# Six different starting addresses for the slots of two weight rings in a two-block forward pass

## The chip, the cores and the metric

The kernel runs on one core of one Trainium2 chip. The metric is device time of one launch in microseconds. One profiled execution is read beside it.

## The reference

Two transformer-like blocks are applied to 256 tokens of width 1024, all in float32. Cut to what matters:

```python
# first block
h = rmsnorm(x, pre_mix_norm);  proj = h @ w_in                 # 1024 x 9792
y_ssd  = ssd_branch(z, xbc, dt, ...) @ w_ssd_out               # conv, two-direction scan, gated norm
y_attn = window_attention(q, k, v, ...) @ w_attn_out
x = x + rmsnorm((g_ssd * y_ssd + g_attn * y_attn) @ w_o)
f = square(relu(rmsnorm(x) @ w_mlp_in)) @ w_mlp_out            # 1024 x 4096, 4096 x 1024
x = x + rmsnorm(f)
# second block
proj = rms_norm(x) @ w_in_2                                    # 1024 x 5120
y_a = neighbourhood_attention(q, k, v) @ w_attn_branch;  y_b = short_gated_conv(cb, cc, ch) @ w_conv_branch
x = x + (sigmoid(ga) * y_a + sigmoid(gb) * y_b) @ w_o
x = x + square(relu(rms_norm(x) @ w_mlp_in)) @ w_mlp_out
```

## The kernel before

All weights come from HBM as 147 pieces (slots 0 to 146 of one list), each 128 partitions by 2048 float32 values, so 8192 bytes in a partition. SyncE fetches them in order into a ring of three tiles `raw`. For each piece ScalarE writes the rounded part `w_hi` (an ACTIVATE with Copy into the type fp32r, line 752), and VectorE writes the rest `w_lo = raw - w_hi` (line 1087). Both parts have a ring of three slots, and piece s uses slot s % 3 of each. ScalarE may write slot s % 3 when TensorE is done with piece s - 3; VectorE and ScalarE are two pieces ahead of TensorE (`AHEAD`).

TensorE takes the pieces in order (`stream`, line 346 in `three`). Each product of full precision is three matmuls in fp32r that add up in PSUM: hi by hi, hi by lo, lo by hi. There are two roles:

- "feat" pieces (q, xbc, mi, cb2, cc2, ch2, mi2 and half of kv): the weights are the stationary operand, 128 by 128, and the activations `ht_hi`/`ht_lo` move, 256 columns. 48 matmuls a piece.
- "tok" and "acc" pieces (z, gate, q2, k2, v2, g2, and ao, so, wo, mo, ab2, cv2, wo2, mo2): the activations are stationary, 128 by 128, and the weights move, 512 columns. 24 matmuls a piece.

The one piece "dt" has stationary weights of 64 columns, eight blocks of 256 bytes one behind the other.

In the profile a matmul is named by its moving operand first: `ps<-ht_hi,w_hi` moves ht_hi over stationary w_hi, and `ps<-w_hi,ff_hi` moves w_hi over stationary ff_hi.

The order of all work is written out by hand in one program per engine, and semaphores are waited for at constants. Every tile in SBUF has an address that is written out too: `at(name, shape, offset)` puts it at that many bytes of a partition beyond a common base, which is 16512 (128 modulo 512). In what follows the residue of a tile is its offset modulo 512; the common base adds the same 128 to all. `raw`, `w_hi`, `w_lo`, `ht_hi`, `ht_lo`, `ot_*`, `yt_*`, `ff_*` and `o2_*` have residue 0, and every block of 128 columns that TensorE takes from them starts at residue 0 again (in "dt" alternately at 0 and 256). `co_hi` and `co_lo`, the gated convolution that is the stationary operand of the two pieces cv2 (slots 109 and 110 of the list), have residue 64: their offsets are 153664 and 157760. These two are the only operands of line 346 that aren't at residue 0.

Of the kernel before, what the change touches and what calls it, by code (L numbers as in the profile page):

```python
# [26 lines left out]
F32R = mybir.dt.float32r  # L27
# [4 lines left out]
P = 128  # L32
TOK = 256
RT = TOK // P
D = 1024
# [6 lines left out]
PER_GROUP = HEADS // GROUPS  # L42
GW = D_INNER // GROUPS
# [4 lines left out]
XROW = TOK + 2 * PAD  # L48
Q_HEADS = 16
# [3 lines left out]
REL_W = 512  # L53
LOG1P_TERMS = 8

HEADS2 = 8
# [3 lines left out]
XROW2 = TOK + 2  # L60

RAW_RING = 3
SPLIT_RING = 3
AHEAD = 2
PIECE = 2048
# [37 lines left out]
PARAM_COLS = sum(w for _, w in PARAMS)  # L103
# [31 lines left out]
def build(nc, w_stream, w_dt, x_in, params_in, table_in, onehot_in, gate_bias_in, post_in, rpb_in,  # L135
# [3 lines left out]
    with ctx:  # L139
# [3 lines left out]
        def at(name, shape, offset, dt=F32):  # L143
            return nc.alloc_sbuf_tensor_at(name, shape, dt, offset=base + offset)

        raw = [at(f"raw{i}", [P, PIECE], 8192 * i) for i in range(RAW_RING)]
        w_hi = [at(f"w_hi{i}", [P, PIECE], 24576 + 8192 * i, F32R) for i in range(SPLIT_RING)]
        w_lo = [at(f"w_lo{i}", [P, PIECE], 49152 + 8192 * i, F32R) for i in range(SPLIT_RING)]

        params = at("params", [P, PARAM_COLS], 73728)  # L150

        def param(name):
            first, width = PARAM_AT[name]
# [12 lines left out]

        quad = param("quad")

        top = [73728 + 4 * PARAM_COLS]

        def scratch(name, shape):
            n = 1
            for s in shape[1:]:
                n *= s
            start = (top[0] + 31) // 32 * 32
            top[0] = start + 4 * n
            return at(name, shape, start)
# [11 lines left out]
        gstat = scratch("gstat", [P, 3, RT * GROUPS])  # L189
        hstat = scratch("hstat", [P, 3, 2 * RT * HEADS2])  # L190
        y_off = scratch("y_off", [P, RT, GW])
        junk = at("junk", [P, GW], 157760)
        assert top[0] <= 83968, top[0]

        ht_hi = at("ht_hi", [P, 8, TOK], 83968, F32R)
        ht_lo = at("ht_lo", [P, 8, TOK], 92160, F32R)
        ot_hi = at("ot_hi", [P, 8, TOK], 100352, F32R)
        ot_lo = at("ot_lo", [P, 8, TOK], 108544, F32R)
        x = at("x", [P, RT, D], 100352)
        g_post = at("g_post", [P, 2, D], 108544)  # L200
        bc = at("bc", [P, 16, TOK], 116736)
        btok = at("btok", [P, RT, 1024], 133120)
        conv_in = [at(f"conv_in{i}", [P, 4, XROW], 141376 + 8256 * i) for i in range(2)]
        conv_acc = [at(f"conv_acc{i}", [P, 4, TOK], 141376 + 8256 * i + 4160) for i in range(2)]
        xtok = at("xtok", [P, RT, D_INNER], 159584)
        dtw = at("dtw", [P, 6, RT, 2 * HEADS], 159584)
        dt_feat = at("dt_feat", [P, TOK], 162656)
        x_first = at("x_first", [P, RT, D], 116736)

        bias1 = at("bias1", [P, Q_HEADS, BIAS_W], 175968)  # L210
        q_t = at("q_t", [P, 8, TOK], 200544)
        k_t = at("k_t", [P, 2, TOK], 208736)
        v_tok = at("v_tok", [P, RT, 256], 210784)
        logit1 = [at(f"logit1_{i}", [P, 4, TOK], 116736 + 4096 * i) for i in range(2)]
        prob_t1 = [at(f"prob_t1_{i}", [P, RT, 4, P], 124928 + 4096 * i) for i in range(2)]
        onehot = at("onehot", [33, REL_W], 133120)
        table = at("table", [33, Q_HEADS], 135168)
        rel_row = at("rel_row", [Q_HEADS, REL_W], 137216)

        zg = at("zg", [P, RT, D_INNER], 175968)  # L220
        gates = at("gates", [P, RT, 2 * D], 192352)
        decay = [at(f"decay{i}", [P, PER_GROUP, P], 141376 + 2048 * i) for i in range(2)]
        step_w = [at(f"step_w{i}", [P, PER_GROUP, P], 145472 + 2048 * i) for i in range(3)]
        step_tmp = at("step_tmp", [P, PER_GROUP, P], 151616)
        cb = at("cb", [P, RT, P], 153664)

        adt_wide = at("adt_wide", [P, 4, 4, HEADS], 175968)
        cum_hi = at("cum_hi", [P, 4, P], 178016, F32R)
# [1 line left out]
        cum_sign = at("cum_sign", [P, 4, P], 182112)  # L230
        cum = at("cum", [P, 4, P], 198496)
        cum_l = [at("cum_l0", [P, 2, PER_GROUP, P], 194400, F32R), at("cum_l1", [P, 2, PER_GROUP, P], 202592, F32R)]
        cum_s = [at("cum_s0", [P, 4, P], 206688, F32R), at("cum_s1", [P, 4, P], 155712, F32R)]
        state = at("state", [P, 2, GW], 208736)
        x_state = at("x_state", [P, 2, GW], 210784)
        yt_hi = at("yt_hi", [P, 16, TOK], 116736, F32R)
        yt_lo = at("yt_lo", [P, 16, TOK], 133120, F32R)

        ff_hi = at("ff_hi", [P, 32, TOK], 116736, F32R)
        ff_lo = at("ff_lo", [P, 32, TOK], 149504, F32R)  # L240
        hn = at("hn", [P, RT, D], 198656)
        ff_tmp = [at(f"ff_tmp{i}", [P, 512], 206848 + 2048 * i) for i in range(2)]

        qk2 = at("qk2", [P, RT, 1024], 116736)
        v2 = at("v2", [P, RT, 512], 124928)
        qk2_t = at("qk2_t", [P, 8, TOK], 129024)
        cb2 = at("cb2", [P, 4, TOK], 137216)
        cc2 = at("cc2", [P, 4, TOK], 141312)
        acc2 = at("acc2", [P, 4, TOK], 145408)
        z2 = at("z2", [P, 4, XROW2], 149504)  # L250
        co_hi = at("co_hi", [P, 4, TOK], 153664, F32R)
        co_lo = at("co_lo", [P, 4, TOK], 157760, F32R)
        logit2 = [at(f"logit2_{i}", [P, 4, TOK], 161856 + 4096 * i) for i in range(2)]
        prob_t2 = [at(f"prob_t2_{i}", [P, RT, 4, P], 170048 + 4096 * i) for i in range(2)]
        bias2 = at("bias2", [P, RT, HEADS2, TOK], 178240)
        gates2 = at("gates2", [P, RT, 2 * D], 194624)
        o2_hi = at("o2_hi", [P, 4, TOK], 108544, F32R)
        o2_lo = at("o2_lo", [P, 4, TOK], 112640, F32R)
        scale_wide = at("scale_wide", [P, RT, P], 198656)
        scale_row = at("scale_row", [P, 2, TOK], 199680)  # L260

        ps = ctx.enter_context(nc.psum_tensor("ps", [P, 8, 512], F32))

# [1571 lines left out]
```

How the kernel before makes its waits and increments, by code:

```python
        def ready(eng, key):  # L307
            eng.wait_ge(*where[key][2])
# [1 line left out]
        def emptied(eng, key):  # L311
            eng.wait_ge(drained[where[key][0]], where[key][1] + 1)
# [13 lines left out]
            def claim(key, b):  # L327
                if uses[b]:
                    pe.wait_ge(drained[b], uses[b])
                where[key] = [b, uses[b], None]
                uses[b] += 1
# [22 lines left out]
            def stream(s):  # L355
                name, form, chunk, part, opens, closes = slots[s]
                hi, lo = w_hi[s % SPLIT_RING], w_lo[s % SPLIT_RING]
                pe.wait_ge(lo_ready, s + 1)
                if form == "acc":
                    a_hi, a_lo = gathered[name]
                    for n in range(2):
# [70 lines left out]
            def norm_turn(j):  # L432
                if j == 0:
                    pe.wait_ge(hn_ready, 2)
                for n in range(2):
                    if j in (1, 2):
                        pe.wait_ge(x_ready, 4 * j - 2 + 2 * n)
                    if j == 3:
                        emptied(pe, ("wo2", n, 0)), emptied(pe, ("wo2", n, 1))
                    turn_pairs(f"norm{j}", x_first if j == 0 else x, 2, 2 * n)
# [1 line left out]
            def mix_turn(j):  # L443
                src = gates if j == 0 else gates2
                for q in range(4):
                    if q % 2 == 0:
                        pe.wait_ge(mixed_ready, 4 * j + 2 * (q // 2 + 1))
                    turn_pairs(f"mix{j}", src, 1, q)
# [49 lines left out]
            def conv_turn(c):  # L499
                pe.wait_ge(conv_silu, c + 1)
                for r in range(RT):
```

## Time and profile before

| | |
|---|---|
| median of 3 runs | 1021.15 us (1018.06 to 1024.70) |
| span of the profiled execution | 1021.7 us |
| TensorE busy | 969.4 us, 95% |
| VectorE, ScalarE, GpSimd busy | 666.1, 524.4, 208.7 us |
| mean granted TensorE clock | 0.975 |
| bytes moved | 166.54 MB, mean 163 GB/s |

The span reaches from the first to the last instruction of the program in the one execution that was profiled; it is 0.6 us above the median of the runs. Matmuls overlap in the pipeline, so the busy time of one (284 or 390 ns) is longer than the distance from its start to the next one's, and only that distance says how fast TensorE works.

### The profile page before, as it was taken

How to read it: one execution, taken by the hardware profiler on the slowest of the kernel's cores; microseconds unless marked ns; L12 is line 12 of the kernel's file. 1: busy time of each engine (PE TensorE's matmuls, PEld its weight loads, DVE VectorE, ACT ScalarE, POOL GpSimd, SP SyncE). 2: the span in 40 equal slices, each digit the busy share in tenths (PEclk: the TensorE clock that was granted, in tenths of full speed). 3: DMA queues.
4: the chain of work that ended last, by engine and by line, in shares of the span. 5: the costliest groups of instructions: out<-in, count | busy, mean ns of one | idle time of the engine just before them, and what ended most of it. 6: DMA issues, size and time to landing. Idle time of an engine off the chain costs nothing.

```text
span 1021.7 us, 13780 instructions
## 1 busy us (share of the span) xinstructions
PE 969.4 (95%) x5726; PEld 849.9 (83%) x5726; DVE 666.1 (65%) x746; ACT 524.4 (51%) x660; POOL 208.7 (20%) x184
## 2 busy tenths in 40 slices
PE   5999998897988999998999999899999999999998
PEld 5997887876766788888999888789988889999887
DVE  4378876978898966467666444686764766565442
ACT  6457885564653564346555433555564345545331
POOL 0005566858887000000000000430000000000000
PEclk9999998998898999998999999899999999999999
DMA  8743223342221538543545555655336345555551
GB/s 314 261 166 120 87 84 124 124 165 62 83 82 52 216 124 302 198 173 140 178 165 192 199 188 205 160 210 181 122 115 233 134 165 206 180 195 200 177 197 41
DMA packets 24974, 166.54 MB, mean 163 GB/s; under 512 B 2938, under 2 KB 3066, under 8 KB 6224
## 3 DMA queue, kind: packets, MB, share of 16 engines
q1 hardware_dynamic: 22320, 156.12, 42.9%
q0 software_dynamic: 2592, 9.54, 3.3%
q8 instruction: 45, 0.74, 0.3%
q14 instruction: 17, 0.14, 0.0%
HBM read 164.57 MB, written 1.08 MB: 162 GB/s over the span
## 4 chain that ended last, share of the span: by engine, by line
PE 72%; DVE 13%; POOL 6%; issue 6%; ACT 3%; DMA 0%; SPq 0%; DVEq 0%; ACTq 0%; POOLq 0%
PE ps L346 65%; DVE w_lo L1087 2%; PE ps L528 2%; POOL conv_acc L1679 2%; POOL y_off L1677 2%; DVE step_w L1303 2%; PE ps L428 2%; DVE conv_acc L1263 2%; POOL logit L1666 1%; DVE decay L1308 1%; DVE xtok L1284 1%; DVE xtok L1340 1%; PE ps L459 1%; PE ps L494 1%; ACT w_hi L752 1%
## 5 line engine op out<-in xcount | busy, mean ns | idle before, releaser
L1087 DVE TENSOR_TENSOR w_lo<-raw,w_hi 128x2048 fp32r<-128x2048 f32 (+1 forms) x147 | 343.5, 2342 | 222.8 <-ACT w_hi L752 222.8
L752 ACT ACTIVATE w_hi<-raw 128x2048 fp32r<-128x2048 f32 (+1 forms) x147 | 279.5, 1904 | 212.9 <-PE ps L346 212.4
L346 PE MATMUL ps<-ht_hi,w_hi 128*128 128x256 f32 x952 | 274.4, 288 | 2.4 <-DVE ht_lo L1125 2.2
L346 PE MATMUL ps<-ht_lo,w_hi 128*128 128x256 f32 x952 | 272.1, 286 | 0.0
L346 PE MATMUL ps<-ht_hi,w_lo 128*128 128x256 f32 x952 | 271.9, 286 | 0.0
L346 PEld LDWEIGHTS ps<-ht_hi,w_hi 128*128 128x128 f32 x952 | 185.0, 194 | 5.5 <-DVE ht_lo L1125 2.8
L346 PEld LDWEIGHTS ps<-ht_lo,w_hi 128*128 128x128 f32 x952 | 185.0, 194 | 0.0
L346 PEld LDWEIGHTS ps<-ht_hi,w_lo 128*128 128x128 f32 x952 | 184.8, 194 | 0.0
L346 PE MATMUL ps<-w_hi,ht_hi 128*128 128x512 f32 (+1 forms) x320 | 126.6, 396 | 0.4 <-DVE w_lo L1087 0.2
L346 PE MATMUL ps<-w_hi,ht_lo 128*128 128x512 f32 (+1 forms) x320 | 123.9, 387 | 0.0
L346 PE MATMUL ps<-w_lo,ht_hi 128*128 128x512 f32 (+1 forms) x320 | 123.9, 387 | 0.0
L346 PE MATMUL ps<-w_hi,ff_hi 128*128 128x512 f32 x256 | 99.8, 390 | 0.0
L346 PE MATMUL ps<-w_lo,ff_hi 128*128 128x512 f32 x256 | 99.7, 390 | 0.0
L346 PE MATMUL ps<-w_hi,ff_lo 128*128 128x512 f32 x256 | 99.7, 390 | 0.0
L346 PEld LDWEIGHTS ps<-w_hi,ht_hi 128*128 128x128 f32 x320 | 60.9, 190 | 12.9 <-issue 0.7
L346 PEld LDWEIGHTS ps<-w_hi,ht_lo 128*128 128x128 f32 x320 | 60.6, 189 | 12.3
L346 PEld LDWEIGHTS ps<-w_lo,ht_hi 128*128 128x128 f32 x320 | 60.9, 190 | 11.8
L346 PEld LDWEIGHTS ps<-w_hi,ff_lo 128*128 128x128 f32 x256 | 48.1, 188 | 10.0
L346 PEld LDWEIGHTS ps<-w_hi,ff_hi 128*128 128x128 f32 x256 | 48.1, 188 | 9.9
L346 PEld LDWEIGHTS ps<-w_lo,ff_hi 128*128 128x128 f32 x256 | 48.1, 188 | 9.8
L1721 POOL MEMSET z<- 128x4 f32 x2 | 0.1, 104 | 253.3 <-PE ps L346 253.3
L1263 DVE SCALAR_TENSOR_TENSOR conv_acc<-conv_in,params,conv_acc 128x256 f32<-128x256 f32 x96 | 48.2, 548 | 1.0
(231 smaller groups left out, 1257.1 us busy)
## 6 DMA issues: line engine op xcount, KB each, us to landing
raw<-in_w_stream SPq DMA_DIRECT2D x146, 1024.0 KB, 4.8
bias<-rel_scratch POOLq DMA_DIRECT2D x1, 3072.0 KB, 16.0
bias<-in_rpb POOLq DMA_DIRECT2D x16, 128.0 KB, 4.2
gates<-in_gate_bias POOLq DMA_DIRECT2D x2, 768.0 KB, 5.0
x_first<-in_x_in SPq DMA_DIRECT2D x2, 512.0 KB, 4.0
x<-in_x_in POOLq DMA_DIRECT2D x1, 1024.0 KB, 7.3
g_post<-in_post POOLq DMA_DIRECT2D x2, 512.0 KB, 10.1
out_y<-x SPq DMA_DIRECT2D x4, 256.0 KB, 2.0
```

The lines of the kernel that those rows point to most:

```text
L346: ins = pe.matmul(o, still, moving, start=first and n == 0, stop=last and n == 2, skip_group_check=True)
L428: ins = pe.transpose(ps[:, b, i * TOK + r * P:i * TOK + r * P + P], source[:, r, f:f + P], ident)
L459: ins = pe.matmul(ps[:, 4 + h // 2, (h % 2) * TOK:(h % 2) * TOK + TOK], qa[rs, (1 - r) * P:(1 - r) * P + P], ka[rs, :], start=True, stop=True)
L494: ins = pe.matmul(ps[e * HD:e * HD + HD, 7, (h // 2) * P:(h // 2) * P + P], v2[:, jt, head * HD:head * HD + HD], prob_t2[a % 2][:, jt, pla ...
L528: ins = pe.matmul(ps[:, 4, o:o + HD], decay[c][:, h, :], xtok[:, c, f:f + HD], start=True, stop=True)
L752: act.activation(w_hi[s % SPLIT_RING][:, 0:width(s)], raw[s % RAW_RING][:, 0:width(s)], ACT.Copy).then_inc(hi_ready, 1)
L1087: dve.tensor_tensor(w_lo[s % SPLIT_RING][:, 0:width(s)], raw[s % RAW_RING][:, 0:width(s)], w_hi[s % SPLIT_RING][:, 0:width(s)].bitcast(F32 ...
L1263: ins = dve.scalar_tensor_tensor(conv_acc[k][:, i, :], conv_in[k][:, i, tap:tap + TOK], conv_w[:, tap, f:f + 1], conv_acc[k][:, i, :], ALU ...
L1284: link(dve.tensor_tensor(v, v, per_head(param("d_skip")[:, 4 * g:4 * g + 4], 4), ALU.mult))
L1303: ins = dve.tensor_tensor(w[:, :, :], w[:, :, :], cb[:, c, :].unsqueeze(1).to_broadcast([P, PER_GROUP, P]), ALU.mult)
L1677: link(pool.tensor_scalar(part, conv_in[k][:, 3, tap:tap + TOK], conv_w[:, tap, f:f + 1], None, ALU.mult))
L1679: ins = pool.tensor_tensor(conv_acc[k][:, 3, :], conv_acc[k][:, 3, :], part, ALU.add)
```

## The change

Only addresses are changed. The instructions of every engine, their order and their waits are the same as before. The slots of `w_hi` start 8256 bytes apart in place of 8192, those of `w_lo` 8288, and `w_lo` begins 192 bytes later. All tiles behind them up to offset 159584 and many beyond it move up by 512 bytes, so their residue stays. In the ring of `raw` nothing changes.

| slot | w_hi before | w_hi now | w_lo before | w_lo now |
|---|---|---|---|---|
| 0 | 0 | 0 | 0 | 192 |
| 1 | 0 | 64 | 0 | 288 |
| 2 | 0 | 128 | 0 | 384 |

The table gives the residues modulo 512. The activations of line 346 stay at 0, and `co_hi`, `co_lo` at 64.

```diff
         raw = [at(f"raw{i}", [P, PIECE], 8192 * i) for i in range(RAW_RING)]
-        w_hi = [at(f"w_hi{i}", [P, PIECE], 24576 + 8192 * i, F32R) for i in range(SPLIT_RING)]
-        w_lo = [at(f"w_lo{i}", [P, PIECE], 49152 + 8192 * i, F32R) for i in range(SPLIT_RING)]
-
-        params = at("params", [P, PARAM_COLS], 73728)
+        w_hi = [at(f"w_hi{i}", [P, PIECE], 24576 + (8192 + 64) * i, F32R) for i in range(SPLIT_RING)]
+        w_lo = [at(f"w_lo{i}", [P, PIECE], 49152 + 192 + (8192 + 96) * i, F32R) for i in range(SPLIT_RING)]
+
+        params = at("params", [P, PARAM_COLS], 74240)
...
-        ht_hi = at("ht_hi", [P, 8, TOK], 83968, F32R)
-        ht_lo = at("ht_lo", [P, 8, TOK], 92160, F32R)
+        ht_hi = at("ht_hi", [P, 8, TOK], 84480, F32R)
+        ht_lo = at("ht_lo", [P, 8, TOK], 92672, F32R)
...
-        ff_hi = at("ff_hi", [P, 32, TOK], 116736, F32R)
-        ff_lo = at("ff_lo", [P, 32, TOK], 149504, F32R)
+        ff_hi = at("ff_hi", [P, 32, TOK], 117248, F32R)
+        ff_lo = at("ff_lo", [P, 32, TOK], 150016, F32R)
...
-        co_hi = at("co_hi", [P, 4, TOK], 153664, F32R)
-        co_lo = at("co_lo", [P, 4, TOK], 157760, F32R)
+        co_hi = at("co_hi", [P, 4, TOK], 154176, F32R)
+        co_lo = at("co_lo", [P, 4, TOK], 158272, F32R)
```

## Rows read from the trace of the kernel before

**Rows 1.** The page, parts 1 and 4: busy time, and the chain by engine

```profile
PE 969.4 (95%) x5726; PEld 849.9 (83%) x5726; DVE 666.1 (65%) x746; ACT 524.4 (51%) x660; POOL 208.7 (20%) x184
...
PE 72%; DVE 13%; POOL 6%; issue 6%; ACT 3%; DMA 0%; SPq 0%; DVEq 0%; ACTq 0%; POOLq 0%
```

**Rows 2.** The chain in order of time: start us, us, what

```profile
23.40 37.47 PE ps L346 x312
...
82.12 1.89 POOL logit L1666
85.01 2.74 POOL conv_acc L1679
...
379.52 55.80 PE ps L346 x246
...
470.93 180.25 PE ps L346 x1152
```

**Rows 3.** Line 346 alone in three stretches: us, PE busy (matmuls), PEld busy, clock, DMA

```profile
0.00:61.00 61.00, 45.30 (x360) 44.92 (x360) 1.00 0.74 274
61.00:343.00 282.00, 156.15 (x985) 140.39 (x985) 0.93 0.30 105
343.00:1021.70 678.70, 634.26 (x3624) 557.50 (x3624) 0.99 0.51 177
```

**Rows 4.** Timeline, TensorE, a "feat" piece of mi: start us, us

```profile
499.86 0.28 PE L346 MATMUL ps<-ht_hi,w_hi 128*128 128x256 f32 x1
...
500.94 0.28 PE L346 MATMUL ps<-ht_hi,w_hi 128*128 128x256 f32 x1
```

**Rows 5.** Timeline, TensorE, pieces ab2: first and last of 48 matmuls

```profile
789.28 0.39 PE L346 MATMUL ps<-w_hi,o_hi 128*128 128x512 f32 x1
...
799.94 0.39 PE L346 MATMUL ps<-w_hi,o_lo 128*128 128x512 f32 x1
```

**Rows 6.** Timeline, TensorE, pieces cv2: the first four and the last of 48

```profile
800.16 0.40 PE L346 MATMUL ps<-w_hi,co_hi 128*128 128x512 f32 x1
800.40 0.39 PE L346 MATMUL ps<-w_lo,co_hi 128*128 128x512 f32 x1
800.63 0.40 PE L346 MATMUL ps<-w_hi,co_lo 128*128 128x512 f32 x1
800.86 0.39 PE L346 MATMUL ps<-w_hi,co_hi 128*128 128x512 f32 x1
...
811.13 0.39 PE L346 MATMUL ps<-w_hi,co_lo 128*128 128x512 f32 x1
```

**Rows 7.** Timeline, TensorE, the piece dt (stationary weights of 64 columns)

```profile
52.57 0.28 PE L346 MATMUL ps<-ht_hi,w_hi 128*64 128x256 f32 x1
...
52.91 0.28 PE L346 MATMUL ps<-ht_hi,w_hi 128*64 128x256 f32 x1
...
53.25 0.28 PE L346 MATMUL ps<-ht_hi,w_hi 128*64 128x256 f32 x1
...
53.59 0.28 PE L346 MATMUL ps<-ht_hi,w_hi 128*64 128x256 f32 x1
```

**Rows 8.** Timeline, TensorE, where the granted clock is 0.5

```profile
170.93 0.42 PE L346 MATMUL ps<-ht_lo,w_hi 128*128 128x256 f32 x1
...
172.00 0.42 PE L346 MATMUL ps<-ht_hi,w_hi 128*128 128x256 f32 x1
```

**Rows 9.** The tiles' own view: ns min/median/max, first and last start

```profile
L752 ACT ACTIVATE w_hi<-raw x147: 621/1916/1962, 8.8 to 1002.3; 128x2048 fp32r<-128x2048 f32 x146, 128x512 fp32r<-128x512 f32 x1
L1087 DVE TENSOR_TENSOR w_lo<-raw,w_hi x147: 692/2292/5094, 10.7 to 1004.2; 128x2048 fp32r<-128x2048 f32 x146, 128x512 fp32r<-128x512 f32 x1
```

**Rows 10.** Waits: who waited for whom, us in total, times, longest

```profile
DVE w_lo L1087 <- ACT w_hi L752: 222.8, 99, 5.9
ACT w_hi L752 <- PE ps L346: 212.4, 74, 4.7
```

More of the change, by code:

```diff
@@ L167, in build @@
         quad = param("quad")
-        top = [73728 + 4 * PARAM_COLS]
+        top = [73728 + 512 + 4 * PARAM_COLS]
         def scratch(name, shape):
@@ L191, in build @@
         y_off = scratch("y_off", [P, RT, GW])
-        junk = at("junk", [P, GW], 157760)
-        assert top[0] <= 83968, top[0]
-        ht_hi = at("ht_hi", [P, 8, TOK], 83968, F32R)
-        ht_lo = at("ht_lo", [P, 8, TOK], 92160, F32R)
[L197 to L204, printed above, removed]
+        junk = at("junk", [P, GW], 158272)
+        assert top[0] <= 83968 + 512, top[0]
+        ht_hi = at("ht_hi", [P, 8, TOK], 84480, F32R)
+        ht_lo = at("ht_lo", [P, 8, TOK], 92672, F32R)
+        ot_hi = at("ot_hi", [P, 8, TOK], 100864, F32R)
+        ot_lo = at("ot_lo", [P, 8, TOK], 109056, F32R)
+        x = at("x", [P, RT, D], 100864)
+        g_post = at("g_post", [P, 2, D], 109056)
+        bc = at("bc", [P, 16, TOK], 117248)
+        btok = at("btok", [P, RT, 1024], 133632)
+        conv_in = [at(f"conv_in{i}", [P, 4, XROW], 141888 + 8256 * i) for i in range(2)]
+        conv_acc = [at(f"conv_acc{i}", [P, 4, TOK], 141888 + 8256 * i + 4160) for i in range(2)]
         xtok = at("xtok", [P, RT, D_INNER], 159584)
@@ L207, in build @@
         dt_feat = at("dt_feat", [P, TOK], 162656)
-        x_first = at("x_first", [P, RT, D], 116736)
+        x_first = at("x_first", [P, RT, D], 117248)
         bias1 = at("bias1", [P, Q_HEADS, BIAS_W], 175968)
@@ L213, in build @@
         v_tok = at("v_tok", [P, RT, 256], 210784)
[L214 to L218, printed above, removed]
+        logit1 = [at(f"logit1_{i}", [P, 4, TOK], 117248 + 4096 * i) for i in range(2)]
+        prob_t1 = [at(f"prob_t1_{i}", [P, RT, 4, P], 125440 + 4096 * i) for i in range(2)]
+        onehot = at("onehot", [33, REL_W], 133632)
+        table = at("table", [33, Q_HEADS], 135680)
+        rel_row = at("rel_row", [Q_HEADS, REL_W], 137728)
         zg = at("zg", [P, RT, D_INNER], 175968)
         gates = at("gates", [P, RT, 2 * D], 192352)
[L222 to L225, printed above, removed]
+        decay = [at(f"decay{i}", [P, PER_GROUP, P], 141888 + 2048 * i) for i in range(2)]
+        step_w = [at(f"step_w{i}", [P, PER_GROUP, P], 145984 + 2048 * i) for i in range(3)]
+        step_tmp = at("step_tmp", [P, PER_GROUP, P], 152128)
+        cb = at("cb", [P, RT, P], 154176)
         adt_wide = at("adt_wide", [P, 4, 4, HEADS], 175968)
@@ L232, in build @@
         cum_l = [at("cum_l0", [P, 2, PER_GROUP, P], 194400, F32R), at("cum_l1", [P, 2, PER_GROUP, P], 202592, F32R)]
-        cum_s = [at("cum_s0", [P, 4, P], 206688, F32R), at("cum_s1", [P, 4, P], 155712, F32R)]
+        cum_s = [at("cum_s0", [P, 4, P], 206688, F32R), at("cum_s1", [P, 4, P], 156224, F32R)]
         state = at("state", [P, 2, GW], 208736)
         x_state = at("x_state", [P, 2, GW], 210784)
-        yt_hi = at("yt_hi", [P, 16, TOK], 116736, F32R)
-        yt_lo = at("yt_lo", [P, 16, TOK], 133120, F32R)
@@ L239, in build @@
-        ff_hi = at("ff_hi", [P, 32, TOK], 116736, F32R)
-        ff_lo = at("ff_lo", [P, 32, TOK], 149504, F32R)
[L241 to L249, printed above, removed]
@@ L250, in build @@
-        z2 = at("z2", [P, 4, XROW2], 149504)
-        co_hi = at("co_hi", [P, 4, TOK], 153664, F32R)
-        co_lo = at("co_lo", [P, 4, TOK], 157760, F32R)
[L253 to L257, printed above, removed]
@@ L258, in build @@
-        o2_lo = at("o2_lo", [P, 4, TOK], 112640, F32R)
-        scale_wide = at("scale_wide", [P, RT, P], 198656)
-        scale_row = at("scale_row", [P, 2, TOK], 199680)
+        yt_hi = at("yt_hi", [P, 16, TOK], 117248, F32R)
+        yt_lo = at("yt_lo", [P, 16, TOK], 133632, F32R)
+        ff_hi = at("ff_hi", [P, 32, TOK], 117248, F32R)
+        ff_lo = at("ff_lo", [P, 32, TOK], 150016, F32R)
+        hn = at("hn", [P, RT, D], 199168)
+        ff_tmp = [at(f"ff_tmp{i}", [P, 512], 207360 + 2048 * i) for i in range(2)]
@@ new lines, in build @@
+        qk2 = at("qk2", [P, RT, 1024], 117248)
+        v2 = at("v2", [P, RT, 512], 125440)
+        qk2_t = at("qk2_t", [P, 8, TOK], 129536)
+        cb2 = at("cb2", [P, 4, TOK], 137728)
+        cc2 = at("cc2", [P, 4, TOK], 141824)
+        acc2 = at("acc2", [P, 4, TOK], 145920)
+        z2 = at("z2", [P, 4, XROW2], 150016)
+        co_hi = at("co_hi", [P, 4, TOK], 154176, F32R)
+        co_lo = at("co_lo", [P, 4, TOK], 158272, F32R)
+        logit2 = [at(f"logit2_{i}", [P, 4, TOK], 162368 + 4096 * i) for i in range(2)]
@@ L262, in build @@
+        prob_t2 = [at(f"prob_t2_{i}", [P, RT, 4, P], 170560 + 4096 * i) for i in range(2)]
+        bias2 = at("bias2", [P, RT, HEADS2, TOK], 178752)
+        gates2 = at("gates2", [P, RT, 2 * D], 195136)
+        o2_hi = at("o2_hi", [P, 4, TOK], 109056, F32R)
+        o2_lo = at("o2_lo", [P, 4, TOK], 113152, F32R)
+        scale_wide = at("scale_wide", [P, RT, P], 199168)
+        scale_row = at("scale_row", [P, 2, TOK], 200192)
         ps = ctx.enter_context(nc.psum_tensor("ps", [P, 8, 512], F32))
```

## The prediction

> **What bounds the kernel now.** I read the page first, for shares: TensorE is busy 95% of the span, and 72% of the chain that ended last runs over it [rows 1]. Then the chain in order of time, for where that holds. From the start to about 61 us and from about 343 us to the end it is nearly nothing but line 346, the matmuls with the streamed weights, in runs such as 1152 matmuls in 180 us [rows 2]. Between 61 and 343 us it goes over GpSimd, VectorE and ScalarE (softmax, convolution, scan) [rows 2], and line 346 is busy only 156 us of 282 there [rows 3]. So a nanosecond more or less on a matmul of line 346 counts in full for 360 + 3624 = 3984 of them and mostly not for the 985 between [rows 3].
>
> Next the splits that fill the two rings. VectorE waits 223 us for ScalarE, and ScalarE 212 us for TensorE to free a slot [rows 10]. Both have slack: a split of a few ns more stays hidden behind TensorE, and one of a few ns less gives nothing.
>
> Last, TensorE's pace, the distance between starts of neighbours. With 256 columns nine steps take 500.94 - 499.86 = 1.08 us, 120 ns each [rows 4]. With 512 columns 47 steps take 799.94 - 789.28 = 10.66 us, 226.8 ns each [rows 5]. At the lower level of the clock (0.5 granted) five steps of 256 columns take 1.07 us, 214 ns each [rows 8]: one column a cycle at 1.2 GHz and nothing on top. At the full clock, 2.4 GHz, the same rule gives 106.7 and 213.3 ns, so each matmul pays **a gap of about 13.4 ns** beyond its columns, whether 256 or 512. In the piece dt, whose stationary blocks are half as wide, three steps take 340 ns, 113.3 each [rows 7]: a gap of 6.7 ns. The gap goes with the width of the weight load that runs beside the matmul, not with the matmul. Something that the stationary and the moving read share costs about a tenth of a nanosecond per loaded column. That is the only place where an address could matter on the chain.
>
> **The change part by part.** *Instructions, waits, DMAs:* none is added, removed or moved, and `raw`, the only target of the weight DMAs, keeps its addresses. These count nothing.
>
> *The splits.* ScalarE's take 1916 ns and VectorE's 2292 in the median, for all three slots together [rows 9]. The nearest rows for another residue don't exist, but the ranges are bounded by slack: of 147 splits, even 100 ns more each would be 15 us against 212 us in which ScalarE waits for TensorE [rows 10]. I take nothing; with the cover gone (61 to 343 us, some 30 splits on VectorE's chain) 100 ns each would be 3 us. A gain there has the same bound, if ScalarE or VectorE now lose time to each other, which the narrow medians speak against.
>
> *The matmuls.* Here the trace has a probe of its own. The pieces ab2 and cv2 follow each other, have the same shape, the same rings and the same clock; only the stationary tiles differ: `o_hi`, `o_lo` at residue 0, `co_hi`, `co_lo` at 64. From the first to the last of cv2, 47 steps take 811.13 - 800.16 = 10.97 us, 233.4 ns each, against 226.8 [rows 5, 6]. The steps alternate between about 0.24 and 0.23 us [rows 6]. **So a shift of 64 bytes between stationary and moving operand costs 6.6 ns a matmul**, half as much again as the gap. It holds through both pieces, whatever the other engines do meanwhile, so I read it as TensorE's two reads hitting each other and not as another engine's traffic.
>
> The second probe is dt. Its stationary blocks start alternately at residue 0 and 256 with the moving operand at 0, and each group of three takes the same 0.34 us [rows 7]. A shift of 256 then costs and gives nothing (with blocks of 64 columns; for 128 it isn't shown).
>
> Now the count. Of the three matmuls of a product two have `w_hi` and one has `w_lo`; over the ring each slot has a third of the pieces. The shift between weights and activations is the slot's residue. Slot 0 of `w_hi` (2/9 of the matmuls) stays at 0 and pays nothing. Slot 1 of `w_hi` (2/9) has 64, the shift of rows 6; as stationary operand it is that very arrangement. `w_lo` has 192, 288, 384 (1/9 each). If what counts repeats every 256 bytes, as dt allows, 192 is 64 on the other side, 288 is 32 and 384 is 128. No row has 32 or 128. So 4/9 of the matmuls (64, 192 and 288) are near the priced case, and 3/9 (128 and 384) may be like it or like 0.
> - at least: 3984 x 4/9 x 6.6 ns = 11.7 us, 1033;
> - at most at this price: 3984 x 7/9 x 6.6 ns = 20.5 us, 1042;
> - taken: half of the undecided 3/9, 3984 x 5.5/9 x 6.6 ns = 16.1 us.
>
> For the cost as such I keep both sides: nothing at all (the 256 of rows 7), and the 13.4 ns of a second gap for the dearest residues, 3984 x 7/9 x 13.4 = 41.5 us. Below nothing: if separate residues took away the gap itself, up to as much the other way. The 48 matmuls of cv2 change too: in slot 109 `w_hi` now has 64 like `co_hi`, the shift is 0 again, and 16 matmuls may drop to 227 ns; 0.1 us.
>
> Sum: 1021.7 (the span) + 16.1 = 1037.8, and the median of the runs stood 0.6 below the span: **1037 us**.
>
> Rows 5 and 6 show 226.8 and 233.4 ns with nothing but the stationary address changed. A rule of the Trainium skill speaks against reading this as a meeting of two reads: its page "SBUF — State Buffer", section "A bandwidth-pool intuition that's wrong (but worth ruling out)", gives TensorE a second, independent read port for weight loads and lets contention come only from a port lock or a starved descriptor generator. By that residues change nothing, and the sum would stay at 1021; the rows disagree. The same page's rule on lines of 16 bytes ("Door 1: The DMA port swizzle") would leave every slot alike too, since all the new offsets are multiples of 16.
>
> **The rivals.**
> *No effect that can be measured.* The cost may be tied to exactly this shift of 64 with the stationary operand ahead. Then only the "feat" pieces in slot 1 pay: 58 whole feat pieces of 48 matmuls, some 45 of them on the chain (2160 matmuls), x 2/9 x 6.6 ns = 3.2 us, 1024. In the tok and acc pieces the weights move, so the shift there has the other sign, which no row shows. For it: dt's indifference. Against it: an arrangement that meets at one offset only would have to be hit by chance by the one odd tile in this kernel. The Trainium skill's two rules above, page "SBUF — State Buffer", come to the same side, at 1021.
> *Faster.* The gap of 13.4 ns is itself the meeting of two reads in step, since before the change both always start at the same residue, and large shifts part them. If the residues from 128 up (`w_hi` slot 2 and all of `w_lo`, 5/9) lose it and slot 1 of `w_hi` (2/9) pays 6.6 ns: -3984 x 5/9 x 13.4 = -29.7, +3984 x 2/9 x 6.6 = +5.8, together -23.8 us, 997; if all six but slot 0 lose it, -41.5 us, 980. It decides if one shift anywhere beats 0. For it: the gap follows the load's width [rows 4, 7] and is gone at the lower clock [rows 8], as a conflict would. Against it: the two shifts that the trace shows, 64 and 256, are worse and equal.
> *Slower by more.* The dearest residues cost a second gap: up to 1021 + 41.5 = 1063.
> *The change doesn't do what it says:* the addresses move as written, but if the conflict is between engines (ScalarE or VectorE writing one slot while TensorE reads another), it could give something; the pace of ab2, cv2 and mi stays flat through splits of both engines, so there is nothing to gain there.
>
> **How the numbers follow.** A cost at about the price of rows 6 on 4/9 to 7/9 of the matmuls: 0.41. A higher price: 0.09. No effect, or one of a few us: 0.30. Faster: 0.20, of which 0.12 near 997 and 0.08 near 980. About 1% (1011 to 1031) is what a measurement can tell from no change here. From the first two cases slower has 0.50, same 0.30, faster 0.20. The range: 1033 to 1042 widened upward to half of the higher price's excess (1054), and down over no effect to the nearer of the faster cases (998); outside lie the rest of faster, 0.14, and of the higher price, 0.04.
>
> **What would show it.** In the profile after, starts on a timeline of mi, mo and mi2: in pieces whose number is 0 modulo 3 the matmuls with `w_hi` keep 120 and 227 ns, in slot 1 they go to about 127 and 233, and those with `w_lo` as well. In cv2 the piece in slot 1 should be faster than before. The splits keep 1916 and 2292 ns, and the stretch from 61 to 343 us keeps its 282 us within 4. I am wrong if line 346 keeps its pace in every slot (no effect), if any slot has a pace below 120 or 227 (a gap that can be removed), or if the splits change by more than 100 ns.

## The result and the profile after

The changed kernel takes 1025.07 us (median of 20 runs, 1021.95 to 1027.36) against 1020.62 us (20 runs, 1017.54 to 1024.70) on the same chips. The ratio is 1.004 with a 95% interval of 1.0027 to 1.0052: slower by 3 to 5 us. I had forecast 1037, so the sign is right and the size is not.

The page after, parts 1 and 4, against [rows 1]:

```profile
PE 967.1 (95%) x5726; PEld 839.4 (82%) x5726; DVE 668.7 (66%) x746; ACT 523.8 (51%) x660; POOL 209.7 (21%) x184
...
PE 71%; DVE 14%; POOL 6%; issue 6%; ACT 3%; DMA 1%; SPq 0%; DVEq 0%; ACTq 0%; POOLq 0%
```

The profiled execution has a span of 1020.4 us, 1.3 below that of before. Single executions of either kernel differ by 5 us and more, and this one had a mean clock of 0.981 against 0.975. Totals are therefore compared by the runs, and the profile by stretches that run at the full clock, or nearly so. The chain in order of time gives such stretches, against [rows 2] (start us, us, what; all of them of 200 or more matmuls). The first one of 1152 matmuls has its first few at the lower clock in some profiles, in that of before for one:

```profile
21.96 37.10 PE ps L346 x312
...
374.19 56.90 PE ps L346 x246
...
467.10 180.39 PE ps L346 x1152
...
753.22 51.60 PE ps L346 x222
...
836.85 180.31 PE ps L346 x1152
```

The first is made of feat pieces, kv and dt, and it is 0.37 us **shorter** than before (37.47). The second is made of acc pieces alone, 246 matmuls of 512 columns, and it is 1.10 us **longer** (55.80), 4.5 ns a matmul. The stretches of 1152 are mi with mo and mi2 with mo2, both kinds. So the change has two effects of opposite sign.

Piece by piece, in slots 0, 1, 2 of mi: first and last of 48 matmuls of 256 columns each, against [rows 4]:

```profile
478.62 0.28 PE L346 MATMUL ps<-ht_hi,w_hi 128*128 128x256 f32 x1
...
484.16 0.28 PE L346 MATMUL ps<-ht_hi,w_lo 128*128 128x256 f32 x1
484.28 0.28 PE L346 MATMUL ps<-ht_hi,w_hi 128*128 128x256 f32 x1
...
489.92 0.28 PE L346 MATMUL ps<-ht_hi,w_lo 128*128 128x256 f32 x1
490.04 0.28 PE L346 MATMUL ps<-ht_hi,w_hi 128*128 128x256 f32 x1
...
495.61 0.28 PE L346 MATMUL ps<-ht_hi,w_lo 128*128 128x256 f32 x1
```

47 steps take 5.54, 5.64 and 5.57 us: 117.9, 120.0 and 118.5 ns a step, where it was 120 in every slot. The same for slots 0, 1, 2 of mo, first and last of 24 matmuls of 512 columns, against [rows 5]:

```profile
564.04 0.40 PE L346 MATMUL ps<-w_hi,ff_hi 128*128 128x512 f32 x1
...
569.31 0.39 PE L346 MATMUL ps<-w_hi,ff_lo 128*128 128x512 f32 x1
569.54 0.39 PE L346 MATMUL ps<-w_hi,ff_hi 128*128 128x512 f32 x1
...
574.84 0.39 PE L346 MATMUL ps<-w_hi,ff_lo 128*128 128x512 f32 x1
575.07 0.40 PE L346 MATMUL ps<-w_hi,ff_hi 128*128 128x512 f32 x1
...
580.44 0.39 PE L346 MATMUL ps<-w_hi,ff_lo 128*128 128x512 f32 x1
```

23 steps take 5.27, 5.30 and 5.37 us: 229, 230 and 233 ns, against 226.8. And cv2, whose stationary operand was always at 64, in slots 1 and 2, against [rows 6]:

```profile
797.70 0.39 PE L346 MATMUL ps<-w_hi,co_hi 128*128 128x512 f32 x1
...
803.02 0.40 PE L346 MATMUL ps<-w_hi,co_lo 128*128 128x512 f32 x1
803.25 0.39 PE L346 MATMUL ps<-w_hi,co_hi 128*128 128x512 f32 x1
...
808.53 0.40 PE L346 MATMUL ps<-w_hi,co_lo 128*128 128x512 f32 x1
```

It has become faster, 231 and 230 ns against 233.4. The splits haven't changed, by the tiles' own view, against [rows 9]:

```profile
L752 ACT ACTIVATE w_hi<-raw x147: 622/1916/1975, 9.2 to 1000.6; 128x2048 fp32r<-128x2048 f32 x146, 128x512 fp32r<-128x512 f32 x1
L1087 DVE TENSOR_TENSOR w_lo<-raw,w_hi x147: 694/2292/5903, 11.2 to 1002.5; 128x2048 fp32r<-128x2048 f32 x146, 128x512 fp32r<-128x512 f32 x1
```

Both medians are the same to the nanosecond.

Taken over the 4968 matmuls of line 346 (distances between neighbours inside a piece at the full clock; waits and the piece dt left out), the mean pace went from 119.9 to 118.7 ns with 256 columns and from 227.1 to 231.3 with 512. On the chain stand 2160 of the first kind and some 1800 of the second: 2160 x -1.2 = -2.6 us, 1800 x 4.2 = +7.6 us, together +5.0. Measured were 4.45, with an interval of about 2.8 to 5.3. The two agree within that interval; what was left was which property of an address counts, and why the two kinds answer with opposite signs.

### The profile page after: what moved, and what is told of

The parts are those of the page before. It is cut to its first block, busy times and chain, and to the rows that moved or that the text cites. A ratio compares the mean times of both kernels' runs of the same rounds, so it can differ in the third digit from the quotient of the medians.

```text
span 1020.4 us, 13780 instructions
## 1 busy us (share of the span) xinstructions
PE 967.1 (95%) x5726; PEld 839.4 (82%) x5726; DVE 668.7 (66%) x746; ACT 523.8 (51%) x660; POOL 209.7 (21%) x184
## 4 chain that ended last, share of the span: by engine, by line
PE 71%; DVE 14%; POOL 6%; issue 6%; ACT 3%; DMA 1%; SPq 0%; DVEq 0%; ACTq 0%; POOLq 0%
PE ps L346 65%; DVE w_lo L1087 3%; POOL conv_acc L1679 2%; PE ps L528 2%; POOL y_off L1677 2%; DVE step_w L1303 2%; DVE conv_acc L1263 2%; POOL logit L1666 1%; PE ps L428 1%; DVE decay L1308 1%; DVE xtok L1284 1%; ACT w_hi L752 1%; DMA raw<-in_w_stream 1%; DVE xtok L1340 1%; PE ps L459 1%
## 5 line engine op out<-in xcount | busy, mean ns | idle before, releaser
L346 PE MATMUL ps<-ht_hi,w_hi 128*128 128x256 f32 x952 | 270.4, 284 | 3.1 <-DVE ht_lo L1125 2.9
L346 PE MATMUL ps<-ht_lo,w_hi 128*128 128x256 f32 x952 | 268.0, 282 | 0.0
L346 PE MATMUL ps<-ht_hi,w_lo 128*128 128x256 f32 x952 | 267.9, 281 | 0.0
L346 PEld LDWEIGHTS ps<-ht_hi,w_hi 128*128 128x128 f32 x952 | 178.9, 188 | 6.0 <-DVE ht_lo L1125 3.3
L346 PEld LDWEIGHTS ps<-ht_lo,w_hi 128*128 128x128 f32 x952 | 179.2, 188 | 0.0
L346 PEld LDWEIGHTS ps<-ht_hi,w_lo 128*128 128x128 f32 x952 | 179.2, 188 | 0.0
L346 PEld LDWEIGHTS ps<-w_hi,ff_hi 128*128 128x128 f32 x256 | 48.1, 188 | 11.2
```

Of the source, the lines that this page charges most:

```text
L346: ins = pe.matmul(o, still, moving, start=first and n == 0, stop=last and n == 2, skip_group_check=True)
```

## The experiments

Theory A says that only the distance between the addresses of TensorE's stationary and moving operand counts, modulo 512. Its rivals are named in the expectations. Every kernel but the last, mo_256, does the whole computation.

**The rings put back, the rest left moved** (c_shift).

```diff
-        w_hi = [at(f"w_hi{i}", [P, PIECE], 24576 + (8192 + 64) * i, F32R) for i in range(SPLIT_RING)]
-        w_lo = [at(f"w_lo{i}", [P, PIECE], 49152 + 192 + (8192 + 96) * i, F32R) for i in range(SPLIT_RING)]
+        w_hi = [at(f"w_hi{i}", [P, PIECE], 24576 + 8192 * i, F32R) for i in range(SPLIT_RING)]
+        w_lo = [at(f"w_lo{i}", [P, PIECE], 49152 + 0 + 8192 * i, F32R) for i in range(SPLIT_RING)]
```

> All six slots of the split weights are back at residue 0, the tiles behind them stay 512 bytes higher. Theory A (TensorE's own two reads meet, so only the distance between stationary and moving address modulo 512 counts): pace as in the kernel before, 120 ns with 256 columns and 226.8 with 512, ratio to before 1.000 (within 0.2%). Theory B (the moved tiles themselves cost something, the rings nothing): ratio 1.004, paces as in the changed kernel, 118.7 and 231.4.

1020.83 us, ratio to before 0.9997 (0.9982 to 1.0012). The same five stretches of its chain:

```profile
23.87 37.47 PE ps L346 x312
...
377.72 55.80 PE ps L346 x246
...
468.79 179.62 PE ps L346 x1152
...
752.62 50.76 PE ps L346 x222
...
835.09 179.47 PE ps L346 x1152
```

37.47 and 55.80 are those of before [rows 2] to the hundredth, and all means are as before (119.9 and 227.1). The tiles moved by 512 bytes cost nothing that can be measured; the rings do it all. Against this control the changed kernel's five stretches add up to -0.37 + 1.10 + 0.77 + 0.84 + 0.84 = +3.2 us for 3084 matmuls.

**A price list** (map_a to map_e). Each slot has one residue in both rings, so its pieces show one distance; everything behind the rings moves by 1024 bytes, and a dump tile (`junk`) into a hole.

```diff
+        ring = (64, 128, 192)
-        w_hi = [at(f"w_hi{i}", [P, PIECE], 24576 + (8192 + 64) * i, F32R) for i in range(SPLIT_RING)]
-        w_lo = [at(f"w_lo{i}", [P, PIECE], 49152 + 192 + (8192 + 96) * i, F32R) for i in range(SPLIT_RING)]
+        w_hi = [at(f"w_hi{i}", [P, PIECE], 24576 + 8192 * i + ring[i], F32R) for i in range(SPLIT_RING)]
+        w_lo = [at(f"w_lo{i}", [P, PIECE], 49152 + 512 + 8192 * i + ring[i], F32R) for i in range(SPLIT_RING)]
```

> Slots 0, 1, 2 of both rings at residues 64, 128, 192, everything behind them 1024 bytes higher than before. A slot has the same residue in w_hi and w_lo, so its pieces show the price of one distance, in both roles. Theory A: every slot has a steady pace of its own; residue 64 with stationary weights is the arrangement of cv2 in the kernel before and costs 6.6 ns, 126.6 in place of 120; ratio to before 1.00 to 1.02. Theory C (an engine's write to one slot meets TensorE's read of another, so only different residues between slots count): slots alike within 1 ns, and equal to the changed kernel, 118.7 and 231.4.

> As map_a with residues 256, 320, 384. Theory A: each slot has a pace of its own; 256 as residue 0 (120 and 226.8), since the piece dt showed no difference between 0 and 256, and if all repeats every 256 bytes, 320 as the 64 of map_a and 384 as its 128. Theory C: slots alike within 1 ns.

> As map_a with residues 32, 96, 448. Theory A: each slot has a pace of its own; with moving weights at 448 the stationary operand is 64 bytes ahead, which is the arrangement of cv2 in the kernel before, so 233.4 ns with 512 columns. Theory C: slots alike within 1 ns.

> Slots at residues 160, 288, 352, for the price list. Theory A with a period of 256: 288 as the 32 of map_c (118.3 and 233.3), 352 as its 96 (118.9 and 233.6), 160 new. Without the period: values of their own.

> Slots at residues 224, 416, 480, for the price list. Theory A with a period of 256: 416 as the 160 of map_d, 480 as 224, and 224 new; with stationary weights one of them may be below the 115.3 of 64 and 448.

The times: map_a 1023.10 us, ratio 1.0023 (1.0002 to 1.0043); map_b 1021.82, 0.9996 (0.9978 to 1.0014); map_c 1026.38, 1.0051 (1.0029 to 1.0074); map_d 1030.85 and map_e 1028.80 in one run each, beside 1019.47 for before. The slots' mean paces in ns, worked out from the traces as above:

| residue of the weights | 0 | 32 | 64 | 96 | 128 | 160 | 192 | 224 |
|---|---|---|---|---|---|---|---|---|
| 256 columns (feat) | 119.9 | 118.3 | 115.4 | 118.9 | 118.7 | 119.9 | 117.6 | 116.9 |
| 512 columns (tok, acc) | 227.1 | 233.3 | 229.2 | 233.6 | 232.4 | 233.9 | 233.3 | 233.3 |

| residue of the weights | 256 | 288 | 320 | 352 | 384 | 416 | 448 | 480 |
|---|---|---|---|---|---|---|---|---|
| 256 columns (feat) | 119.8 | 118.3 | 116.8 | 118.3 | 118.7 | 120.0 | 115.3 | 116.8 |
| 512 columns (tok, acc) | 227.9 | 233.2 | 229.7 | 233.3 | 232.6 | 234.0 | 233.1 | 233.3 |

How such a number comes out of rows: map_a, slot 0 (residue 64), the piece of mi and the piece of mo, first and last matmul each.

```profile
484.31 0.28 PE L347 MATMUL ps<-ht_hi,w_hi 128*128 128x256 f32 x1
...
489.64 0.28 PE L347 MATMUL ps<-ht_hi,w_lo 128*128 128x256 f32 x1
...
568.19 0.39 PE L347 MATMUL ps<-w_hi,ff_hi 128*128 128x512 f32 x1
...
573.46 0.39 PE L347 MATMUL ps<-w_hi,ff_lo 128*128 128x512 f32 x1
```

5.33 us in 47 steps are 113.4 ns, 5.27 in 23 are 229.1. (This piece of mi is faster than its slot's mean; see below.)

Slots differ steadily, by up to 4.6 ns in their means, where the theory of writes of one engine meeting reads of another (C) wanted them alike within 1 ns; ht_64 below, with all slots at residue 0, leaves no room for it. The list repeats after 256 bytes, within 0.8 ns with 512 columns. With 256 columns it does so within 0.6 ns but for two pairs, 64 and 320 (115.4 and 116.8) and 192 and 448 (117.6 and 115.3). There single pieces ran at different steady paces, and the list has their mean: 113.3 and 117.8 at 64 (map_a), 320 (map_b) and 448 (map_c), nearly always 117.8 at 192, and 117.3 to 120.0 at 96. No distance is cheaper than 0 with 512 columns, and none is dearer than 0 by more than 0.1 ns with 256. With stationary weights nothing in map_e fell below the 115.3 of 448, as I had thought possible. That it is the distance, and not the residue of the weight tile, is told by cv2, whose stationary tile is at 64: with weights at 128, 192, 320, 384, 96 and 448 it ran at 229.6, 232.7, 228.5, 229.6, 233.2 and 232.3 ns, and the list has 229.2, 232.4, 227.9, 229.7, 233.3 and 232.6 at 64 less. My expectation for residue 64 with stationary weights, 126.6 ns, was wrong: it is 115.4.

The list also rebuilds the changed kernel. Two of three matmuls have `w_hi`, one `w_lo`: slot 1 with 512 columns should be (2 x 229.2 + 233.2) / 3 = 230.5, and is 230.8; slots 0 and 2 give 229.2 and 232.5, and are 229.9 and 233.0. With 256 columns it holds less well, 119.1, 116.4 and 118.7 against 117.8, 119.6 and 118.7: there the two kinds of matmul in one piece seem not to add up.

Two more things are in these traces. At the lower clock the distance makes no difference. Here is slot 0 of map_a, at 64, in a stretch whose granted clock is 0.5:

```profile
16.86 0.42 PE L347 MATMUL ps<-ht_hi,w_lo 128*128 128x256 f32 x1
...
19.64 0.41 PE L347 MATMUL ps<-ht_hi,w_hi 128*128 128x256 f32 x1
```

13 steps take 2.78 us, 213.8 ns each, which is the pace of [rows 8] at distance 0. And the piece dt, with its 64 stationary columns, can go the other way from the feat pieces at the full clock: 113.7 ns at distance 0, 116.7 at 32 (map_c) and 119.0 at 64, from the first to the last of its 24 matmuls in map_a:

```profile
52.64 0.28 PE L347 MATMUL ps<-ht_hi,w_hi 128*64 128x256 f32 x1
...
55.37 0.28 PE L347 MATMUL ps<-ht_hi,w_lo 128*64 128x256 f32 x1
```

At a distance of 64 the piece dt has 118.9 ns in ht_64 below too, but 113.3 in feat_64 and in the repeat of ht_64.

**The activations moved, not the weights** (ht_64).

```diff
-        ht_hi = at("ht_hi", [P, 8, TOK], 84480, F32R)
-        ht_lo = at("ht_lo", [P, 8, TOK], 92672, F32R)
+        ht_hi = at("ht_hi", [P, 8, TOK], 84480 - 64, F32R)
+        ht_lo = at("ht_lo", [P, 8, TOK], 92672 - 64, F32R)
```

The rings are those of c_shift.

> The rings are at residue 0; ht_hi and ht_lo alone start 64 bytes lower, at residue 448. Theory A (only the distance between TensorE's two reads counts, with the price list of map_a to map_c): feat pieces go from 120 to 115.4 ns (2160 matmuls on the chain, -9.9 us), the tok pieces and wo, wo2, whose stationary operand is ht, from 227 to 229.2 (some 620 on the chain, +1.4 us), all other acc pieces stay at 227. Together -8.5 us, ratio 0.992. Theory D (the residue of the weight tile itself, or of its writers, makes the pace): all paces as before, ratio 1.000.

**Only the feat pieces' weights moved** (feat_64). The slots get 16 columns more, and a feat piece starts at column 16 unless it would reach into a neighbouring slot that starts at 0. The split and the matmuls take the piece through `piece_of_slot`.

```diff
+        def begin(s):
+            if not feat(s):
+                return 0
+            near = [n for n in (s - 2, s + 1) if 0 <= n < SLOTS] if s % 3 < 2 else []
+            return 16 if all(begin(n) for n in near) else 0
+
+        def piece_of_slot(t, s, n):
+            return t[:, begin(s):begin(s) + n]
```

> The slots of both rings have room for 16 columns more, and a feat piece starts 64 bytes into its slot, the others at 0; 13 of the 61 feat, kv and dt pieces stay at 0, where they would reach into a neighbour. Theory A: the shifted feat pieces run at 115.4 ns, everything else as before; some 34 x 48 matmuls on the chain x 4.5 ns = -7.3 us, ratio 0.993. Theory D as theory A here. A third theory, that a faster TensorE only waits longer for the splits and pieces: ratio above 0.997 with the same paces.

ht_64 takes 1007.37 us against 1019.47, ratio **0.9881** (0.9858 to 0.9905), and feat_64 1013.38, ratio 0.9937 (0.9912 to 0.9962). With the residues of both rings at 0, theory D, that the tile's own residue makes the pace, is gone. In ht_64 the feat pieces have a mean of 115.3 ns, the tok pieces with wo and wo2 229, the other acc pieces 227 (cv2 keeps its 233), as expected; the gain of 12 us is larger than the 8.5 us of the list. feat_64 leaves the acc pieces at 227.1 and brings the feat pieces to 117.1. The shifted ones among them have a mean of 116.2, with those of mi and mi2 at 117.8, and not the 115.4 that I expected. Both gains reach the time, so nothing waits for the splits in TensorE's place.

Where the surplus lies is seen in the chain of ht_64, the same five stretches:

```profile
21.96 36.57 PE ps L346 x312
...
371.28 55.80 PE ps L346 x246
...
462.37 175.22 PE ps L346 x1152
...
740.17 51.09 PE ps L346 x222
...
823.15 177.79 PE ps L346 x1152
```

From the start of the first stretch to its end, and from the start of the second to the end of the last, ht_64 is 0.9 and 7.2 us ahead of c_shift, together 8.1: that is the list's 8.5. Another 3.6 us lie between the first two stretches (312.75 us against 316.38), the part that I had left out of the count, where 15 of the 16 xbc pieces are; the last 1.9 lie before the first. Neither is a firm number: the same part between takes 318.65 us in the profile of before, whose paces are those of c_shift. In the repeat of this kernel below the list's 8.5 us lie inside the interval.

The two stretches of 1152 are the same work at the same addresses (mi with mo, mi2 with mo2), and they differ by 2.6 us. All of it is in the feat half: every one of the 16 pieces of mi runs at 113 ns, every one of mi2 at 118 (q and others at either); the first few matmuls of mi, at the lower clock, hide a part of the difference. So at this distance there are **two steady paces**, and in mi and mi2 a stretch keeps the one it has fallen into. The slot at 64 in map_a has the same split, 113 in mi and 118 in mi2.

**Does chance choose between the two?** (ht_64b, the same kernel again), **and is the other side of 0 better?** (ht_up and best, with ht 64 bytes higher; best also moves those weights that meet ht as stationary operand.)

```diff
-        ht_hi = at("ht_hi", [P, 8, TOK], 84480, F32R)
-        ht_lo = at("ht_lo", [P, 8, TOK], 92672, F32R)
+        ht_hi = at("ht_hi", [P, 8, TOK], 85056, F32R)
+        ht_lo = at("ht_lo", [P, 8, TOK], 93248, F32R)
```

85056 and 93248 have residue 64; the tiles before and behind are moved by 512 and 1024 to make room. best has in addition the `begin` of feat_64, for tok pieces and wo, wo2.

> The kernel of ht_64 once more, for a second profiled execution. There the same addresses ran at two steady paces: 113 ns in mi, 118 in mi2 and q. Theory E (which of the two a stretch falls into depends on how its first reads meet, so on chance): other stretches at 113 and 118 in this profile, ratio again between 0.985 and 0.992. Theory F (something fixed in the program sets it): mi at 113 and mi2 at 118 again. If one price of 115.4 held, ratio 0.992.

> The rings are at residue 0, ht_hi and ht_lo 64 bytes higher, so that the stationary weights lie 64 bytes below the moving operand, the 448 of map_c, which ran at 113 ns in mi and mi2 both. If that holds: feat pieces 113 to 115.3 (2160 on the chain, -9.9 to -14.9 us); tok pieces and wo, wo2 from 227 to 233.1 (some 620, +3.8 us). Together -6 to -11 us, ratio 0.989 to 0.994. Theory without signs (only the size of the distance counts): tok at 229.2 as in ht_64, ratio 0.988 or below.

> As ht_up, and the pieces whose stationary operand is ht start 64 bytes into their slot (23 of 38; the others would reach into a neighbour that starts at 0, and stay at 233). By the price list: feat as in ht_up, 23 of the 38 at 227, the 15 others at 233 (14 of them on the chain, 336 matmuls, +2.0 us): -8 to -13 us, ratio 0.987 to 0.992, and 0.998 to 0.999 of ht_up.

ht_64b: 1011.90 us, ratio 0.9898 (0.9866 to 0.9929). Its two stretches:

```profile
467.78 174.99 PE ps L346 x1152
...
829.76 177.79 PE ps L346 x1152
```

mi at 113 and mi2 at 118 again, which speaks for something fixed (F). But q ran at 114 here and at 118 in ht_64, and the two pieces of kv had 113 and 118 in this profile and 118 and 114 in that one: there it changes from execution to execution (E). The runs of this kernel spread over 9 us (1005.46 to 1014.58), against 7 us for before. Neither theory holds alone.

ht_up: 1017.95 us, ratio 0.9967 (0.9947 to 0.9987). The tok pieces, wo and wo2 are at 233, as the list says for 448, so the sign of the distance counts with 512 columns. The feat pieces are at 118 nearly throughout, not at the 113 that 448 had in mi and mi2 of map_c:

```profile
469.15 178.34 PE ps L347 x1152
...
837.19 177.78 PE ps L347 x1152
```

best: 1013.35 us, ratio 0.9920 (0.9895 to 0.9944); feat at 118 again, 23 of the 38 moved pieces back at 227 to 229. It beats ht_up; against ht_64b, beside which it ran, the intervals overlap. My hope that the fast pace belongs to 448 was wrong, and which of the two a stretch takes stays open.

**Is it the role of the weights or the number of columns?** (mo_256.) Feat and acc pieces differ in both. The 24 matmuls of a piece of mo and mo2 become 48 of 256 columns, over the same tiles in the same roles. In this kernel the start flag is set for the second half of a bank as well as for the first, so its sums aren't those of the other kernels; the matmuls, their operands and their order are complete.

```diff
+                                parts = 2 if name in ("mo", "mo2") else 1
+                                for q in range(parts):
+                                    w = 512 // parts
+                                    c = slice(cols.start + q * w, cols.start + q * w + w)
-                                ins = three(ps[:, b, :], a_hi[:, k, r * P:r * P + P],
-                                            a_lo[:, k, r * P:r * P + P], hi[:, cols], lo[:, cols],
+                                    ins = three(ps[:, b, q * w:q * w + w], a_hi[:, k, r * P:r * P + P],
+                                                a_lo[:, k, r * P:r * P + P], hi[:, c], lo[:, c],
...
```

> Slots 0, 1, 2 of both rings at residues 0, 64, 128, and in mo and mo2 each matmul of 512 columns is two of 256, with the same tiles, the same roles and twice the weight loads. Theory G (the number of moving columns decides whether a shift gains or costs): with 256 columns the moving weights pay 120 ns in slot 0, and less in slots 1 and 2, 113 to 118 and about 118.7, as the feat pieces do at these distances. Theory H (the role decides: moving weights pay for a shift, stationary ones gain): slot 0 at 120, slots 1 and 2 above it by 1 to 3 ns. The time itself is longer than before either way: 768 pairs at 2 x 120 in place of 227 ns, +10 us or so.

The pieces of mo in slots 0, 1 and 2 (residues 0, 64, 128), first and last of 48:

```profile
570.75 0.28 PE L347 MATMUL ps<-w_hi,ff_hi 128*128 128x256 f32 x1
...
576.38 0.28 PE L347 MATMUL ps<-w_hi,ff_lo 128*128 128x256 f32 x1
576.50 0.28 PE L347 MATMUL ps<-w_hi,ff_hi 128*128 128x256 f32 x1
...
582.04 0.28 PE L347 MATMUL ps<-w_hi,ff_lo 128*128 128x256 f32 x1
582.16 0.28 PE L347 MATMUL ps<-w_hi,ff_hi 128*128 128x256 f32 x1
...
587.74 0.28 PE L347 MATMUL ps<-w_hi,ff_lo 128*128 128x256 f32 x1
```

47 steps take 5.63, 5.54 and 5.58 us: 119.8, 117.9 and 118.7 ns. With 512 columns the same distances cost 2 and 5 ns more than 0; with 256 they save 2 and 1. The number of columns decides (G), not the role (H). The kernels with the whole computation have a place of this kind too: in the second half of a kv piece the weights move in 256 columns. In ht_64b these steps took 113.4 ns in one kv piece and 118.0 in the other, against 120 in before. The time of mo_256, 1031.18 us in one run beside 1024.65, is longer, as expected with twice the matmuls in mo and mo2; the 6.5 us stand on one run each.

## Why the prediction was off

- **What bounds the kernel** was right: line 346 on 3984 matmuls, the splits with slack. The price of a matmul reached the time in both directions.
- **"Nothing" for instructions, moved tiles and splits** was right: c_shift has a ratio of 0.9997, and the splits have the same medians. The argument from narrow medians was a weak one, since [rows 9] show VectorE's splits from 692 to 5094 ns; it is the result that shows it.
- **The cost of a distance**, from cv2, was right for what it was read from: the arrangement of cv2 returns with the weights moved (233.1 at 448), and cv2 gained when its distances changed. That the sum's average fits the half with 512 columns, 5.5/9 x 6.6 = 4.0 ns a matmul against a measured 4.2, is luck in part. There 64 costs 2.1 ns (229.2), not 6.6, since the sign of the distance counts and cv2 has the stationary operand ahead; the prediction says that no row shows this sign, and gives it the price all the same. 128 and 384 cost 5.3 and 5.5 ns where the sum took 3.3. The two errors nearly cancel.
- **The step that failed** is "as stationary operand it is that very arrangement": I gave the price of a matmul of 512 columns to those of 256. They are more than half of the chain's matmuls, and they gain 1.2 ns in place of paying 4.0. That is 2160 x 5.2 ns = 11.2 us, most of the 12 between 1037 and 1025. Both kinds of pace stood in the rows of before, but only one of them with a second distance, since cv2 has none with 256 columns; the bound below nothing that I kept for the whole belonged here, to this half. One of my own signs of being wrong came true: slots with a pace below 120 (117.9 and 118.5 in mi).
- **The undecided residues** (128 and 384) both turned out dear with 512 columns, 232.4 and 232.6. The dt piece's indifference to 256 was a true sign: the list repeats after 256 bytes, as said above. What I expected by kind of matmul, `w_hi` in slot 0 at 120 and 227 still, did not hold: in slot 0 of mo the three kinds of step take 230.4, 230.6 and 229.3 ns, so the price of `w_lo` is spread over its neighbours.
- **The gap "goes with the width of the weight load"** holds at distance 0 alone: at 64 the dt piece, with half the width, takes 119 or 113.3 ns, and the feat pieces 113.3 or 117.8.
- **The rival "faster"** had the direction that holds with 256 columns, a gap that shrinks when the operands are moved apart: from 13.4 to 6.6 ns in the fast pace at 64. It had put the gain at 128 and beyond and a cost at 64, and the list has 118.7 and 115.4. What I held against it was the row at 64, which has 512 columns, and dt's at 256. Its 997 us asked for it on both kinds.
- **The rule of the Trainium skill** that I weighed (page "SBUF — State Buffer", section "A bandwidth-pool intuition that's wrong (but worth ruling out)": a second, independent read port for weight loads, contention only by a port lock or a starved descriptor generator) would have given 1021, with the same pace at every address. The runs show something else: from 115 to 120 and from 227 to 234 ns by address alone. Whether the two reads meet at a port they don't tell.

## What to carry over

A price read from a trace holds for the shape that it was read from; before it is spread over other shapes, ask whether any row shows the same factor there, and if not, give that share its own bounds on both sides. In this kernel, which TensorE bounds with fp32r matmuls and their weight loads, the distance between the two operands' addresses is a free knob, to be set per shape: 0 for 512 columns and 64 bytes for 256. The two numbers changed in ht_64 give 64 to the matmuls of 256 columns and leave 0 to most of those of 512, and that kernel is 1.0 to 1.2% faster than before (0.9881, and 0.9898 when run again), while spreading the slots over six residues is 0.4% slower. Slots that share one residue are not a fault in themselves.

## What the runs showed of the hardware

- Each fp32r matmul with a 128-column weight load beside it pays about 13.4 ns beyond its columns at 2.4 GHz, with its two operands at distance 0, and none at 1.2 GHz [rows 4, 5, 8], there at a distance of 64 neither (213.8 ns, map_a). At 2.4 GHz that gap depends on the distance modulo 256 between the stationary and the moving operand's address: 14 to 21 ns with 512 columns, 6.6 to 13.4 with 256. What inside the chip makes it so no run here tells.
- At a distance of 64 there are two steady paces with 256 columns, 113.3 and 117.8 ns. mi2 took the slow one in both profiles of ht_64 and mi the fast one; the short stretches q and kv changed between executions. At 448 and 96 (map_c) pieces of one slot also ran at different steady paces. What sets them is open.
- With 64 stationary columns in place of 128 (the piece dt) the pace is 113.7 ns at 0, and at 64 it is 119 in two profiles (map_a, ht_64) and 113.3 in two others (feat_64, ht_64b).
- Engines that write one slot while TensorE reads another don't slow it: in the acc pieces of the kernel before, cv2 left out, more than 9 of 10 steps lie between 226 and 228 ns. Their mean is 227.0 ns with no split beside them, 226.8 beside ScalarE's and 226.7 beside VectorE's.
